# Block 3: gated sums of the first two token tiles onto the residual as accumulating transfers

## The reference, cut to what matters

```
h = rmsnorm_3(x, norm1_g[l]) * (1.0 + sc1) + sh1
y = hybrid_mixer_3(h, ...)          # ends with: return merged @ w_out
x = x + gt1 * y
h = rmsnorm_3(x, norm2_g[l]) * (1.0 + sc2) + sh2
x = x + gt2 * (jnp.square(jax.nn.relu(h @ mlp_w1[l])) @ mlp_w2[l])
return rmsnorm_3(x, final_g)
```

## Time and profile before

| what | us |
|---|---|
| median of 3 runs | 3423.39 |
| lowest and highest | 3422.58 and 3426.14 |
| span of the profiled execution, first to last instruction | 3420.3 |
| PE busy, share of the span | 3348.4, 98% |
| DVE busy | 2278.8, 67% |
| ACT busy | 1593.4, 47% |
| POOL busy | 339.6, 10% |
| transfers, mean over the span | 113 GB/s |

### The profile page before, as it was taken

How to read it: one execution, slowest core, us unless ns; L and a number is a source line. 1 busy time by engine, 2 the same in 40 slices (tenths; PEclk the granted TensorE clock), 3 DMA queues, 4 the chain that set the end, 5 groups by cost and what they waited for, 6 DMA issues and landing times. The chain is left out here.

```text
span 3420.3 us, 48737 instructions
## 1 busy us (share of the span) xinstructions
PE 3348.4 (98%) x18576; PEld 2856.2 (84%) x18576; DVE 2278.8 (67%) x3709; ACT 1593.4 (47%) x2932; POOL 339.6 (10%) x375
## 2 busy tenths in 40 slices
PE   8999999999999999999999999999999999999999
PEld 7998888877788899887887888888787888889987
DVE  6887474778447787853565576667465567678865
ACT  3565254454433455555324363346355243355654
POOL 1000200022010100022010100000000104222200
PEclk9999999999999999999999999999999999999999
DMA  6346312220334435520454242245410330142464
GB/s 218 109 149 206 111 49 64 91 69 25 104 102 137 157 108 170 173 73 25 160 161 143 75 134 97 96 165 168 122 38 26 109 99 26 38 148 81 136 200 157
DMA packets 107988, 386.48 MB, mean 113 GB/s; under 512 B 12060, under 2 KB 14764, under 8 KB 107504
## 3 DMA queue, kind: packets, MB, share of 16 engines
q1 hardware_dynamic: 101088, 364.86, 32.6%
q0 software_dynamic: 4528, 16.43, 1.5%
q10 hardware_dynamic: 2144, 2.10, 0.2%
HBM read 379.13 MB, written 4.21 MB: 112 GB/s over the span
## 5 line engine op out<-in xcount | busy, mean ns | idle before, releaser
L445 DVE TENSOR_TENSOR w_low<-ring,w_high 128x1024 fp32r<-128x1024 f32 (+1 forms) x481 | 591.3, 1231 | 496.3 <-ACT w_high L433 490.6
L433 ACT ACTIVATE w_high<-ring 128x1024 fp32r<-128x1024 f32 (+1 forms) x481 | 485.0, 1010 | 491.8 <-PE bank L469 212.8
L469 PE MATMUL bank<-x_low,w_high 128*128 128x512 f32 (+1 forms) x1712 | 654.9, 388 | 19.5 <-DVE w_low L445 13.0
L469 PE MATMUL bank<-x_high,w_low 128*128 128x512 f32 (+1 forms) x1712 | 641.4, 380 | 0.0
L469 PE MATMUL bank<-x_high,w_high 128*128 128x512 f32 (+1 forms) x1712 | 417.8, 381 | 0.0
L469 PEld LDWEIGHTS bank<-x_low,w_high 128*128 128x128 f32 x1712 | 323.1, 189 | 82.4 <-issue 17.6
L469 PEld LDWEIGHTS bank<-x_high,w_low 128*128 128x128 f32 x1712 | 323.4, 189 | 56.9 <-issue 3.6
L469 PEld LDWEIGHTS bank<-x_high,w_high 128*128 128x128 f32 x1712 | 304.6, 189 | 59.1 <-issue 4.8
L738 PE MATMUL bank<-w_low,x_high 128*128 128x512 f32 (+1 forms) x384 | 145.6, 379 | 3.6 <-ACT z_z L2102 1.5
L740 PE MATMUL bank<-w_high,x_high 128*128 128x512 f32 (+1 forms) x384 | 143.5, 374 | 0.0
L739 PE MATMUL bank<-w_high,x_low 128*128 128x512 f32 (+1 forms) x384 | 143.5, 374 | 0.0
(11 more groups left out here) (821 smaller groups left out, 8215.0 us busy)
## 6 DMA issues: line engine op xcount, KB each, us to landing
ring<-in_W SPq DMA_DIRECT2D x686, 512.0 KB, 3.5
X<-in_x POOLq DMA_DIRECT2D x1, 2048.0 KB, 9.7
x_spill<-X POOLq DMA_DIRECT2D x1, 2048.0 KB, 8.2
X<-x_spill POOLq DMA_DIRECT2D x4, 512.0 KB, 3.5
ring<-in_W SPq DMA_DIRECT2D x4, 432.0 KB, 4.0
out<-X SPq DMA_DIRECT2D x3, 512.0 KB, 5.5
const<-in_consts POOLq DMA_DIRECT2D x1, 1133.0 KB, 10.6
f_hid<-in_xT ACTq DMA_DIRECT2D x4, 256.0 KB, 8.2
```

What stands on the lines that cost most here:

```text
L433: ac.activation(b.UH[u.place][:, 0:u.K * u.n], u.src(), ACT.Copy).then_inc(*b.split.act.up("high", i))
L445: dv.tensor_tensor(b.UL[u.place][:, 0:n], u.src(), b.UH[u.place][:, 0:n].bitcast(F32), SUB).then_inc(*b.split.dve.up("low", i))
L469: i = pe.matmul(out, w[:, k, c], v, start=n == 0 and q == 0, stop=last and q == 3 * K - 1)
```

## The change

At both places, for t = 0 and t = 1, GpSimd no longer adds. It issues, for each half, a transfer from `tmp[h]` to X that adds onto what lies there (`accum_op=ADD`), 128 rows of 2 KB, 256 KB. Its completion raises the semaphore `x` by 16, which before only the load of the input used. `gated_added` gives the value at which both halves of tile t have landed: 16 for the load, 32 for each tile, so 48 and 80 at the first place and 112 and 144 at the second. DVE's multiplications of tiles 1 and 2 and ACT's squares of tiles 0 and 1 wait for that value in place of GpSimd's semaphore. Each half of tile 1 thus waits for both halves of tile 0, where it waited for its own half. Tiles 2 and 3 stay as they were.

```diff
     for h in halves:
         dv.wait_ge(*g.pe.at(tag, "row", t, h))
         if t:
-            dv.wait_ge(*g.pool.at("sum", t - 1, h))
+            dv.wait_ge(*(g.pool.at("sum", t - 1, h) if t == 3 else gated_added(b, g, t - 1)))
         dv.tensor_tensor(tmp[h], b.bk[tag, t, h], GT[:, h * 512:(h + 1) * 512], MUL).then_inc(*g.dve.up("part", t, h))
...
         b.nc.gpsimd.wait_ge(*g.dve.at("part", t, h))
-        b.nc.gpsimd.tensor_tensor(x, x, tmp[h], ADD).then_inc(*g.pool.up("sum", t, h))
-
-
-def gated_summed(g, t):
+        if t < 2:
+            b.nc.gpsimd.dma_start(x, tmp[h], accum_op=ADD).then_inc(b.load_sem("x"), 16)
+        else:
+            b.nc.gpsimd.tensor_tensor(x, x, tmp[h], ADD).then_inc(*g.pool.up("sum", t, h))
+
+
+def gated_added(b, g, t):
+    at = 32 * t + (112 if g.pe.name.startswith("final") else 48)
+    return b.load_sem("x"), at
+
+
+def gated_summed(b, g, t):
+    if t < 2:
+        return [gated_added(b, g, t)]
     return [g.pool.at("sum", 3, 0), g.dve.at("sum")] if t == 3 else [g.pool.at("sum", t, 1)]
```

More of the change, by code:

```diff
@@ L4530, in scalar_final @@
     ac, g = b.nc.scalar, s.gf
-    for w in gated_summed(g, t):
+    for w in gated_summed(b, g, t):
         ac.wait_ge(*w)
@@ L4540, in scalar_final_last @@
     ac, g = b.nc.scalar, s.gf
-    for h, w in enumerate(gated_summed(g, 3)):
+    for h, w in enumerate(gated_summed(b, g, 3)):
         c = slice(512 * h, 512 * h + 512)
@@ L4822, in scalar_gated_end @@
             for t in at.at(k, 1):
-                scalar_rms_square(b, turn, t, gated_summed(g, t))
+                scalar_rms_square(b, turn, t, gated_summed(b, g, t))
             for t in at.at(k, 2):
```

## The result

The changed kernel takes 3441.35 us, median of 4 runs (3437.77 to 3443.47); the kernel before, run beside it, took 3424.14 us (4 runs, 3422.58 to 3426.14). The ratio is 1.0047, with a 95% interval of 1.0036 to 1.0059: about 17 us slower, where 5.4 were forecast and 3438.0 was the top of the range.

A forecast was written before the change was run, and what follows sets the result against it. PE, busy 98% of the span, was taken as the bound, so only moved pauses count: 5.36 us at the first place plus 0 at the second, on 3423.39, gave 3428.8 us (+0.16%), range 3423.5 to 3438.0.

The forecast's parts named there:

- the first place's chain: From tile 1's sum through ACT and DVE to PE's row at 3063.47: 4.94 us without slack, delay forecast +5.36 us.
- Relief: Rival, first place: PE's 1.18 us pause is DVE's load, so up to 1.18 comes back: 3422.6 us; chance 0.04.
- The catching up between the tiles: Rival, first place: ACT catches up, only tile 0's 2.81 us less 1.15 of slack shows: 3425.1 us; chance 0.03.
- C = 5.0: Time from POOL's second issue of a pair to the start of who waits for the landing, taken as 5.0 us.
- C0 + C1 - 4.64: First place's cost formula, with C0 and C1 the issue-to-waiter times of tiles 0 and 1; forecast 5.36 us.
- The rival of slow transfers: Adding transfers behave like four times the bytes: 7.4 us to the waiter, first place 10.16, kernel 3436.1 us; chance 0.27.
- C - 6.15: Second place: what each of the two tiles costs once C passes 6.15 us; forecast 0 us at C = 5.0.
- the cover: Second place: slack before PE starts unit 6, 1.15 us left at C = 5.0, gone when C passes 6.15.
- A held issue: Rival, first place: DVE's scaling holds up tile 1's second issue by up to 0.8 us: 3429.6 us; chance 0.06.
- The rule for such transfers: Skill page's price for a GpSimd-issued transfer, 2.6 us for 256 KB; by it the sum would be +0.6 us.
- the rival of light transfers: An addition lands like a lone plain 256 KB transfer, 3.1 us; first place costs 1.56, kernel 3425.0 us; chance 0.17.

The follow-up runs named there:

- copies with the weights held: Changed kernel with plain copies in place of adding transfers and four MLP weight loads held until first-place transfers landed: 3427.98 us, ratio 1.0009.
- tile 0 alone: Changed kernel with only tile 0 of both places added by transfer, tile 1 by POOL as before: 3431.68 us, ratio 1.0015.
- second place only: Changed kernel with transfers only at the second place (`final`), POOL adding at the first as before: 3429.23 us, ratio 1.0013.
- one transfer per tile: Changed kernel with one adding transfer of 512 KB per tile in place of two of 256 KB, both places: 3435.64 us, ratio 1.0031.
- tile 1 only: Changed kernel with only tile 1 of both places added by transfer, tile 0 by POOL as before: 3430.14 us, ratio 1.0016.
- copies: Changed kernel with the same transfers without the addition, residual left out in tiles 0 and 1: 3432.00 us, ratio 1.0020.
- weights held back: Changed kernel with SP holding four MLP weight loads until the first place's adding transfers had landed: 3437.53 us, ratio 1.0037.
- the kernel with the first place alone: Changed kernel with transfers only at the first place (`out3`), POOL adding at the second as before: 3435.50 us, ratio 1.0030.

## Why the prediction was wrong

**The bound and the first place's chain held.** The prediction said that the first place costs what the two squares are late, with no slack between tile 1's square and PE. In D that is D0 + D1 - 7.31, less the sum before. With 3.52 + 3.79 = 7.31 it gives 10.34 for the changed kernel, measured 10.37; over the other eight kernels that touch this place it gives 10.66, 5.93, 4.22, 7.93, 4.53, 4.81, 1.34 and -2.29 (in the order of the table), against 10.65, 5.92, 4.20, 7.91, 4.56, 4.78, 1.33 and -2.13. The row that stood at 3063.47 is at 3076.96, later by 13.49, which is 3.15 + 10.34. Relief is out with that: DVE's parts were fast again and gave nothing, and the copies with the weights held, whose D grew by 1.34 in sum, lost 1.33. The catching up between the tiles is out too: tile 0 alone costs 5.92, all of its 5.96 us of D.

**The step that failed is C = 5.0**, "because that row is nearest: also 256 KB, also the last of a group on this queue, also waited for, and with weights streaming beside it". In the changed kernel POOL's second issues begin at 3052.5 and 3065.5, in both cases 0.6 to 0.7 us behind the first, so the issue went nearly as forecast (0.57) though each lasts 0.9 to 1.5 us. C, from there to ACT's squares at 3060.34 and 3072.05, is 7.85 and 6.55. By the prediction's own formula C0 + C1 - 4.64 that is 9.8 of the 10.37; the rest is in the steps ahead of it, from DVE's product to POOL's first issue (1.00 and 0.98 us, before 0.76 and 0.77) and on to the second. The row from POOL's queue stood for the bytes and the neighbours, but not for what an adding transfer does on the engines: 1.65 us of all sixteen where the same bytes copied take 0.65, which the prediction covered with the words that the 512 KB and 256 KB ahead of it in that row stand for it. The runs show two causes, each 3.2 to 3.5 us on the two tiles and more than additive together: the adding, and the weights that share the engines. The weights' own share was read well enough: over 3064 to 3072 the engines are 0.72 and 0.89 busy, 6.4 us, of which two additions take 3.3 by the price above, and what is left, 0.39 of the time, is little more than the 0.33 of the earlier trace rows.

**The rival of slow transfers had the size right at the first place**: C = 7.4 and 10.16 us, for measured 7.85 and 6.55, and 10.37 us. The sum is that close partly by luck, since one C is above 7.4 and the other below. Its reason, an adding transfer like one with four times the bytes, is too strong by the engine time: 2.5 times a copy. It took 3436.1 for the kernel and had the second place too small, at 2.5 us.

**At the second place the step that failed is that each tile pays alone**, C - 6.15 each. C here was 7.4 and 7.6 (POOL's second issues begin at 3343.17 and 3360.49), by which the formula gives 2.7 us, for a measured 4.85; so the cover was passed, which the prediction had named as a sign of being wrong, and it was passed by more than C explains. Let L be a tile's lateness, D less its value before: 4.81 and 4.94 in the changed kernel. DVE's product of tile 1 came 17.32 us after that of tile 0 (3358.92 - 3341.60), before 13.64:

```profile
3341.78 1.28 DVE L4337 TENSOR_TENSOR f_relu<-bank,m_gate 128x512 f32<-128x512 f32 x2
```

so 3.68 of tile 0's 4.81 was still there: from the square's wait on, DVE works off its parts back to back and reaches the product late. In all seven kernels in which tile 0 was late here, L0 less that carry is 1.12 to 1.14. In these kernels the square of tile 1 is then late by L0 - 1.13 + L1, and with tile 0 on time by L1. What PE loses is the larger of this and L0, less a lead of 3.75 us (the prediction had 3.32):

| kernel | tile 1's square late | less 3.75 | measured |
|---|---|---|---|
| after | 8.62 | 4.87 | 4.85 |
| second place only | 7.92 | 4.17 | 4.17 |
| one transfer per tile | 7.06 | 3.31 | 3.31 |
| tile 1 only | 5.47 | 1.72 | 1.72 |
| copies, weights held | 4.46 | 0.71 | 0.70 |
| copies | 3.57 | below 0 | 0.00 |
| tile 0 only (L0 = 4.52) | 2.70 | 0.77, by L0 | 0.82 |
| weights held back | 8.53 | 4.78 | 5.37 |

The rule and its lead of 3.75 were drawn from these rows after the fact, and one of them fixes the lead; the six others that fit are evidence. The last row is 0.59 off, and it is the only one of these kernels in which PE fell to its lower level at this place. PE's row and the window behind it:

```profile
3366.98 0.79 PE L855 MATMUL bank<-f3s_unit,f3d_in 128*128 128x512 f32 x1 [3.27 <-DVE f3d_in L832]
```

```profile
3364.00:3368.00 4.00, 1.02 (x3) 0.83 (x4) 1.13 (x3) 3.19 (x7) 0.00 (x0) 0.80 0.05 22
3368.00:3372.00 4.00, 4.00 (x15) 3.23 (x14) 3.96 (x7) 2.84 (x5) 0.00 (x0) 0.77 0.41 131
```

Here there is no next stop at which PE would have waited anyway, as there is at the first place. That this is the 0.59 fits, but wasn't tried by itself.

**A held issue** is not what happened, at this size: the longest issue, 1.53 us in tile 1's pair, does lie beside DVE's scaling, which took its least time of 0.76 (at 3065.30). But tile 1's C is the shorter of the two, and in the kernel with one transfer per tile the issue at 3062.72 took 0.86 us against 0.93 at 3050.35. The two were never set apart by themselves; the 0.27 us between the pairs' issue times, 2.12 and 1.85, bounds what it can have been here.

**The rule for such transfers**, which the prediction set beside its own figure: the Trainium skill, DMA: Bandwidth & Descriptors, Anatomy of one DMA, gives 2.0 us plus the bytes at 436 GB/s, by which an estimate for 256 KB is 2.6 us. The copies with the weights held landed in 2.3 to 2.9 us at the first place, and there this case agrees. With the weights beside them copies took 3.4 to 5.1, and additions 4.2 to 7.8, to which the rule's two terms do not speak. So the rival of light transfers holds for a copy on engines free of weights, and for no addition here.

**Details.** PE's pauses at the first place were forecast to grow by 5.4 us in sum. They grew by 6.22 (from 1.97 to 8.19) and the place by 10.37. The rest, 4.15 us, is in the matmuls behind the pauses, most of them at the lower clock; that PE was slow there is also why the last pause of the earlier trace rows is gone. It is no cost on top: the chain formula, which knows of no clock, gives 10.34, and it fits as well in the copies and with the weights held (4.53 for 4.56, 4.81 for 4.78), where the granted clock stayed at 1.00 at this place. What PE lost by running slowly it would have waited at its next stop. The squares came 8.52 and 7.15 us after POOL's first issues, for a forecast of 5.6. ACT's idle time before tile 1's square was 6.54 us; the prediction's "about 5" is 4.7 by its own sum (2.18, and 5.36 less 2.81). The transfers didn't hold up the weights so far that PE stood: each of its pauses at both places ends in an input part from DVE (L829), none in a load.

## What to carry over

A transfer that adds, put into a chain of waits in place of a small addition, has to be priced on the engines as it will meet them: here its landing took from 3.4 us, with them free of weights, to 8.5 beside weights (in the kernel with the first place alone), and it held them 2.5 times as long as the same bytes copied. When two such delays share one lead, count what of the first is still there when the second begins (at the second place all but 1.13 us of it) before taking off the lead, and take the lead off once. Where an engine idles in such a chain, another with time to spare can do the addition in its order, as DVE did here in 2.5 us for both products and both sums of a tile.

## What the chip showed that was not expected

- A transfer of 256 KB that adds from SBUF onto SBUF is 144 packets and 1.65 us of all sixteen engines (copied: 80 packets, 0.65 us). As one of 512 KB it is 72 packets per 256 KB and 1.5 us (17.4% of 35 us over two, halved).
- POOL's issue of it takes 0.85 to 1.53 us where a plain one takes 0.54 to 0.68, but the second of a pair begins 0.6 to 0.7 us behind the first all the same.
- PE fell to its lower level behind most of its longer pauses, and matmuls of 128x512 then came 0.43 us apart in place of 0.23. At the two places, over all kernels, it fell behind pauses of 2.83, 3.15 (twice), 3.27, 3.31, 3.80, 4.08, 4.15 and 4.88 us, within three matmuls, and not behind 2.38 (the copies), 2.85 (the changed kernel's second place) and 3.48 (the weights held back, first place; the windows from 3064 to 3080 all show 1.00):

```profile
3071.07 0.50 PE L855 MATMUL bank<-o_place,o_in 128*128 128x512 f32 x1 [3.48 <-DVE o_in L832]
```

So the length of the pause alone doesn't decide it. At the first place the lower level cost nothing beyond the chain, at the second perhaps the 0.59 us above.

- Executions differ ahead of the change. DVE's product of tile 0 at the first place, behind 3048 us of work that no edit touches, started at 3047.67 before and at 3048.21 to 3054.26 in the others, 3.15 us late in the changed kernel. Some 2 us of this come up around 2400 us; here are windows of before and then of the changed kernel:

```profile
2360.00:2380.00 20.00, 18.17 (x90) 14.89 (x89) 14.48 (x23) 13.34 (x25) 0.00 (x0) 1.00 0.57 182
```

```profile
2360.00:2380.00 20.00, 18.22 (x77) 14.54 (x76) 12.56 (x22) 12.19 (x22) 0.00 (x0) 0.91 0.48 174
```

The granted clock was 0.91 in place of 1.00 there, and again from 2400 to 2420 us. The same rows of PE stood 1.13 us later than before ahead of the first dip (2371.26 for 2370.13) and 2.71 behind it (2389.60 for 2386.89), and DVE's row at 2414.38 stood 4.12 later behind the second (before 2410.26). The kernel before then paused 1.22 us for weights at 2421.32, where the changed one did not, which takes 0.9 back. The pauses ahead of the dips were no longer than before: 1.78 us ahead of the first (before 1.83), and 1.72 and 0.87 ahead of the second (before 1.72 and 0.86). The two places explain 15.2 of the 17.2 us between the medians; the other 2.0 are of the size of this scatter, and the interval of the ratio, 12 to 20 us, holds both. Why the clock dips there in some executions stays open.
